# Recurrent gates' pieces before the branch gates' piece, and the first softmax beside the last piece, in a two-layer hybrid decoder on one core

## The reference, cut to what matters

```python
h = x @ W_in            # one projection, columns for all head groups
y = concat([
  nsa_mixer(...),       # 4 heads: compressed + selected + sliding branch, mixed by g = sigmoid(gate_logit)
  sliding_window(...),  # 4 heads with sinks (SWA)
  hgrn2_mixer(...),     # 4 recurrent heads; o = o * rsqrt(mean(o*o) + eps) * norm_g * silu(hg)
]) @ W_out
# compressed branch: blocks = t[:, tok] + cmp_pos ; silu(blocks.reshape(n, 32*64) @ w1) @ w2, for k and for v
```

## Time and profile before

| | |
|---|---|
| median of 3 runs | 2209.33 us (2207.95 to 2210.56) |
| profiled execution, own time | 2208.09 us |
| its span, first to last instruction | 2206.2 us |
| PE busy | 2176.4 us (99%) |
| DVE busy | 1133.1 us (51%) |
| ACT busy | 903.0 us (41%) |
| granted TensorE clock | 1.000 |

### The profile page before, as it was taken

The page is one execution under the profiler, slowest core; times in us unless marked ns, Lnnn a source line. Parts: engine busy times, 40 slices in busy tenths (PEclk is TensorE's granted clock), DMA queues, the critical chain, the costliest instruction groups (busy, mean ns, idle before and its releaser), DMA issues.

```text
span 2206.2 us, 30817 instructions
## 1 busy us (share of the span) xinstructions
PE 2176.4 (99%) x12675; PEld 1801.2 (82%) x12675; DVE 1133.1 (51%) x1968; ACT 903.0 (41%) x1449; POOL 137.5 (6%) x128
## 2 busy tenths in 40 slices
PE   9999999999999999999999999999999999999999
PEld 7888888887668888888888888898876788888888
DVE  4333344898857333343643333358988663333454
ACT  4223223656646322222532222256576463222244
POOL 0000011220000000011000000112200100000110
PEclk9999999999999999999999999999999999999999
DMA  5333333332223333332333333333322233333332
GB/s 169 99 101 97 89 96 91 100 79 58 82 72 87 96 96 96 102 94 85 102 96 97 100 99 87 98 82 100 86 75 62 60 104 96 96 96 105 89 89 72
DMA packets 384220, 202.76 MB, mean 92 GB/s; under 512 B 17361, under 2 KB 381777, under 8 KB 384081
## 3 DMA queue, kind: packets, MB, share of 16 engines
q1 hardware_dynamic: 383520, 200.15, 31.9%
q10 hardware_dynamic: 560, 0.66, 0.1%
HBM read 198.68 MB, written 2.10 MB: 91 GB/s over the span
## 4 chain that ended last, share of the span: by engine, by line
PE 92%; ACT 4%; DVE 3%; issue 1%; DMA 1%; POOL 0%; SPq 0%; DVEq 0%; ACTq 0%
PE banks L254 27%; PE banks L256 27%; PE banks L255 27%; ACT xhi L353 1%; PE banks L1524 1%; ACT xT L354 1%; PE banks L1511 1%; PE banks L1465 1%; PE banks L311 1%; PE banks L305 1%; PE banks L1008 1%; PE banks L306 1%; ACT w_hi L240 0%; PE banks L1012 0%; ACT lev L1720 0%
## 5 line engine op out<-in xcount | busy, mean ns | idle before, releaser
L246 DVE TENSOR_TENSOR w_lo<-w_raw,w_hi 128x1024 fp32r<-128x1024 f32 (+2 forms) x370 | 451.0, 1222 | 814.2 <-ACT w_hi L240 814.0
L254 PE MATMUL banks<-xhi,w_hi 128*128 128x512 f32 (+1 forms) x1936 | 757.2, 391 | 1.5 <-DVE w_lo L246 1.5
L256 PE MATMUL banks<-xhi,w_lo 128*128 128x512 f32 (+1 forms) x1936 | 748.9, 387 | 0.0
L255 PE MATMUL banks<-xlo,w_hi 128*128 128x512 f32 (+1 forms) x1936 | 748.7, 387 | 0.0
L240 ACT ACTIVATE w_hi<-w_raw 128x1024 fp32r<-128x1024 f32 (+2 forms) x370 | 375.9, 1018 | 811.8 <-PE banks L256 796.5
L254 PEld LDWEIGHTS banks<-xhi,w_hi 128*128 128x128 f32 x1936 | 365.0, 189 | 75.9 <-DVE w_lo L246 2.0
L256 PEld LDWEIGHTS banks<-xhi,w_lo 128*128 128x128 f32 x1936 | 363.5, 188 | 74.4
L255 PEld LDWEIGHTS banks<-xlo,w_hi 128*128 128x128 f32 x1936 | 363.8, 188 | 72.7 <-issue 1.0
L254 PE MATMUL banks<-hhi,w_hi 128*128 128x512 f32 (+1 forms) x792 | 293.4, 371 | 0.0
L256 PE MATMUL banks<-hhi,w_lo 128*128 128x512 f32 (+1 forms) x792 | 289.5, 365 | 0.0
L255 PE MATMUL banks<-hlo,w_hi 128*128 128x512 f32 (+1 forms) x792 | 289.4, 365 | 0.0
(11 more groups left out here) (276 smaller groups left out, 1990.8 us busy)
## 6 DMA issues: line engine op xcount, KB each, us to landing
w_raw<-in_ffn_w_gu_dram SPq DMA_DIRECT2D x176, 512.0 KB, 3.9
w_raw<-in_ffn_w_down_dram SPq DMA_DIRECT2D x64, 512.0 KB, 4.0
w_raw<-in_w_in_dram SPq DMA_DIRECT2D x48, 512.0 KB, 4.1
w_raw<-in_ffn_w_down_dram SPq DMA_DIRECT2D x32, 384.0 KB, 3.5
w_raw<-in_w_out_dram SPq DMA_DIRECT2D x32, 256.0 KB, 2.9
w_raw<-in_ple_gate_w_dram SPq DMA_DIRECT2D x16, 512.0 KB, 3.8
w_raw<-in_cmp_k_w_dram SPq DMA_DIRECT2D x16, 256.0 KB, 2.8
w_raw<-in_cmp_v_w_dram SPq DMA_DIRECT2D x16, 256.0 KB, 3.1
```

What stands on the lines that cost most here:

```text
L246: dve.tensor_tensor(part_view(wlo, n), raw_view(split_at[n]).rearrange("p k n -> p (k n)"), part_view(whi, n), ALU.subtract).then_inc(sems ...
L254: pe.matmul(bank, w_hi, x_hi, start=first, stop=False)
L255: pe.matmul(bank, w_hi, x_lo, start=False, stop=False)
L256: return pe.matmul(bank, w_lo, x_hi, start=False, stop=last)
```

## The change

`ORDER` puts the four recurrent-gate pieces at s = 21 to 24 and the branch-gate piece last (s = 25), so ACT moves out s = 21 and DVE moves out s = 25. The gates' tiles move to `lev` 0 to 3. `cut_blocks` runs two steps sooner (s = 21 and 22), as the Silu table's load does by one (s = 22). Three eighths stand before piece 24, three before piece 25 (after `scores(0)`), and two after it; before, two stood before piece 25 and six after it. `gated` of heads 0 to 2 comes in steps 24 and 25. ACT goes from the root of head 3 to the exponentials of unit 0 with no table load between; `scores(1)` comes first after piece 25, in the banks of unit 0. The branch gates' transposes come in turn 1, moved out by a plain copy; their tanh comes in turn 5. Four chunks of eight come sooner, from turns (5, 6, 7, 12, 16, 18, 20, 22) to (2, 4, 6, 7, 12, 15, 18, 21), with the splits of their weights, and chunk 0 waits for each head's part by itself.

```diff
-         T_HI + 3, T_CMP, T_SQ, T_SQ + 1, T_SK, T_Q, T_Q + 1, T_KK, T_VV, T_SV, T_GATE, T_HG, T_HG + 1,
-         T_HG + 2, T_HG + 3]
+         T_HI + 3, T_CMP, T_SQ, T_SQ + 1, T_SK, T_Q, T_Q + 1, T_KK, T_VV, T_SV, T_HG, T_HG + 1, T_HG + 2,
+         T_HG + 3, T_GATE]
...
         def gate_of(h):
-            return lev[:, (0, 1, 12, 13)[h], :]
+            return lev[:, h, :]
...
             for s in range(3, N_IN):
+                if s == N_IN - 2:
+                    pe.wait_ge(*upto("blk_done", layer, 2))
+                    for e in range(3):
+                        eighth(pe, layer, e)
                 if s == N_IN - 1:
                     pe.wait_ge(*upto("rope_out", layer, 3))
                     pe.wait_ge(*upto("swapped", layer, 2))
                     scores(pe, layer, 0)
-                    pe.wait_ge(*upto("blk_done", layer, 2))
-                    eighth(pe, layer, 0)
-                    eighth(pe, layer, 1)
+                    for e in range(3, 6):
+                        eighth(pe, layer, e)
                     square_mean(H - 1)
...
-                if s == LATE:
-                    pe.wait_ge(*upto("b4_out", layer, 4 * H + 1))
-                    projected(pe, layer, T_GATE)
-                    for c in range(QT):
-                        mm = pe.transpose(...)
-                    mm.then_inc(sems["gate_turned"], 1)
...
-                if s == LATE:
+                if s == LATE - 1:
                     act.preload_act_table_set("silu_and_others")
...
-                if s == LATE + 1:
-                    act.wait_ge(*upto("gate_turned", layer, 1))
-                    act.activation(gates[:], src, ACT.Tanh, scale=0.5).then_inc(sems["gates_in"], 1)
...
                 if s == N_IN - 1:
                     act.preload_act_table_set("natural_log_exp_and_others")
                     root(act, layer, H - 1)
-                    act.preload_act_table_set("silu_and_others")
-            act.preload_act_table_set("natural_log_exp_and_others")
+                    exponentials(act, layer, 0)
...
-                if s in (LATE, LATE + 1):
-                    cut_blocks(s - LATE)
-            for g in range(H - 1):
-                gated(dve, layer, g)
+                if s in (LATE - 2, LATE - 1):
+                    cut_blocks(s - LATE + 2)
+                if s == LATE + 1:
+                    gated(dve, layer, 0)
+                    gated(dve, layer, 1)
+                if s == LATE + 2:
+                    gated(dve, layer, 2)
             scaled_head(dve, layer, H - 1)
...
-        CMP_TURNS = {-1: (2, 3), 0: (4,), 1: (5,), 2: (6,), 3: (7,)}
+        CMP_TURNS = {-1: (6, 7)}
+        GATE_TURN = 1
-        HG_HI = {0: (0,), 1: (1,), 2: (2,), 3: (3,)}
-        HG_LO = {1: (0,), 2: (1,), 3: (2,), 4: (3,)}
-        CHUNK_TURNS = (5, 6, 7, 12, 16, 18, 20, 22)
-        SPLIT_TURNS = (3, 4, 5, 10, 14, 16, 18, 20, 21, 22, 23, 24)
+        HG_HI = {0: (0, 1), 1: (2, 3)}
+        HG_LO = {1: (0, 1), 2: (2, 3)}
+        CHUNK_TURNS = (2, 4, 6, 7, 12, 15, 18, 21)
+        SPLIT_TURNS = (0, 2, 4, 5, 10, 13, 16, 19, 21, 22, 23, 24)
...
         def score_bank(n):
-            return 2 - 2 * (n % 2)
+            return 2 if n == 0 else 2 * (n % 2)
...
-            if n >= 2:
+            if n == 1:
+                pe.wait_ge(*upto("exp_done", layer, 1))
+            if n >= 3:
                 pe.wait_ge(*upto("exp_done", layer, n - 1))
-            if n == 1:
+            if n == 2:
                 pe.wait_ge(*chunk_out(layer, N_IN - 1))
                 pe.wait_ge(*chunk_out(layer, N_IN - 2))
...
                 if c == 0:
                     pe.wait_ge(*upto("ms_out", layer, H))
-                    pe.wait_ge(*upto("hg_lo", layer, 4))
...
+                def head_there(k):
+                    pe.wait_ge(*upto("hg_lo", layer, k + 1))
+                multiply(pe, w0 + c, 7, ..., ready=None if c else head_there)
...
+            scores(pe, layer, 1)
             compressed(-1)
             for n in range(UNITS + 4):
                 if n >= 4:
                     values(n - 4)
-                if n + 1 < UNITS:
+                if 0 < n < UNITS - 1:
                     scores(pe, layer, n + 1)
...
+                if n == GATE_TURN:
+                    act.wait_ge(*upto("gate_turned", layer, 1))
+                    act.activation(gates[:], src, ACT.Copy).then_inc(sems["gates_raw"], 1)
                 if n == HID_ACT - 1:
                     act.preload_act_table_set("exp_and_others")
+                    act.wait_ge(*upto("gates_raw", layer, 1))
+                    act.activation(gates[:], gates[:], ACT.Tanh, scale=0.5).then_inc(sems["gates_in"], 1)
```

More of the change, by code:

```diff
@@ L123, in build @@
                 "rope_swap": 24, "rope_step": 6, "rope_out": 6, "swapped": 4,
-                "sv_turned": 1, "sv_out": 1, "gate_turned": 1, "gates_in": 1, "hg_gated": 4, "hg_hi": 4, "hg_lo": 4,
+                "sv_turned": 1, "sv_out": 1, "gate_turned": 1, "gates_raw": 1, "gates_in": 1, "hg_gated": 4, "hg_hi": 4, "hg_lo": 4,
                 "cmp_mm": 8, "hid_odd": 1, "hid_sum": 1, "hid_act": 1, "hid_dve": 1, "hid_turned": 1, "hid_out": 1, "vc_zero": 1, "kc_mm": 1, "kc_out": 6,
@@ L1102, in out @@
                 if gate_:
-                    act.wait_ge(*upto("c_mm", layer, (3 if ORDER[s] < T_HG + 2 else 4) * QT))
+                    act.wait_ge(*upto("c_mm", layer, 3 * QT))
                 act.activation(chunk_tile(s), ps[:, chunk_bank(s), :], ACT.Silu if gate_ else ACT.Copy).then_inc(sems["out_act"], 1)
@@ L1483, in row_max, with exponentials @@
                 dve.tensor_scalar(nb2, m2, -SCALE, None, ALU.mult).then_inc(sems["nb_ready"], 1)
+        def exponentials(act, layer, n):
+            kind, w_ = units[n][0], width(n)
+            act.wait_ge(*upto("nb_ready", layer, n + 1))
+            if n == 1:
+                act.wait_ge(*upto("c_mm", layer, STEPS))
+            if n == 2:
+                act.wait_ge(*upto("hg_gated", layer, H))
+            if kind == SWA:
+                act.activation(e_sink[:, n % 2, :], e_sink[:, n % 2, :], ACT.Exp)
+            for hh in range(2):
+                e = act.activation(prob[n % 3][:, hh, 0:w_], ps[:, score_bank(n) + hh, 0:w_], ACT.Exp, scale=SCALE,
+                                   bias=nb[:, n % 2, hh:hh + 1], accum_out=sums[:, n % 2, hh:hh + 1])
+            e.then_inc(sems["exp_done"], 1)
         def eighth(pe, layer, e):
@@ L1505, in turn @@
                     evicted(n - 1)
+                if n == 0:
+                    pe.wait_ge(*upto("gates_raw", layer, 1))
                 if n == SWA_N:
@@ L1537, in compressed @@
                     eighth(pe, layer, e)
+                if n == GATE_TURN:
+                    pe.wait_ge(*upto("b4_out", layer, 4 * H + 1))
+                    projected(pe, layer, T_GATE)
+                    for c in range(QT):
+                        mm = pe.transpose(ps[:, 4, 32 * c:32 * c + 32], proj[0:32, T_GATE, tokens(c)], ident[0:32, 0:32])
+                    mm.then_inc(sems["gate_turned"], 1)
                 if n == HID_TURN:
-                    pe.wait_ge(*upto("half_done", layer, 3))
+                    pe.wait_ge(*upto("half_done", layer, 4))
                     pe.wait_ge(*upto("hid_dve", layer, 1))
@@ L1563, in compressed @@
                     pe.wait_ge(*upto("pc_done", layer, 1))
-                    pe.wait_ge(*upto("half_done", layer, 4))
+                    pe.wait_ge(*upto("half_done", layer, 5))
                     for u4 in range(4):
@@ L1572, in chunk @@
                     pe.wait_ge(*upto("ms_out", layer, H))
-                    pe.wait_ge(*upto("hg_lo", layer, 4))
                 elif n == SC_TURN + 1:
                     pe.wait_ge(*upto("sc_sub", layer, 1))
-                elif n == PCT_TURN + 2:
+                elif n == PCT_TURN + 1:
                     pe.wait_ge(*upto("pct_out", layer, 1))
@@ L1708, in heads_act @@
                     src = turned_both(m) if units[m][0] == SWA else ps[:, 4:6, 0:width(m)]
-                    if m == 2:
-                        act.wait_ge(*upto("hg_gated", layer, 4))
                     act.activation(prob_t[:, m % 3, :, 0:width(m)], src, ACT.Copy).then_inc(sems["ev_act"], 1)
@@ L1713, in heads_act @@
                     out_hi(ENDS.index(n - 4))
[L1714 to L1722, removed]
+                if 0 < n < UNITS:
+                    exponentials(act, layer, n)
                 between(n)
@@ L1765, in between @@
                     gated(dve, layer, g)
-                if n == 5:
+                if n == HID_ACT:
                     open_gates(dve, layer)
```

6 lines of the change are left out of this document (3 added, 3 removed).

## The result

The change makes the kernel 3.9 us slower: a median of 2213.06 us (2212.28 to 2214.94) against 2209.14 (2207.5 to 2212.45), 16 runs each, ratio 1.0017 with an interval of 1.001 to 1.0025. The direction was the forecast one; the forecast was +5.5.

A forecast was written before the change was run, and what follows sets the result against it. PE is busy 99% of the span, so only its waits count. New waits of 5.85 us a layer, less those removed, gave +2.25 and +3.25, together +5.5: 2214.8 us, range 2208 to 2218.5, likeliest case 2212 to 2217.

The forecast's parts named there:

- Part 1: Before piece 24: eighth 0 waits for DVE's two cuts, late from table load and Silu; 1.05 us a layer.
- Part 2: Eighths 3 to 5 before piece 25: PE waits for their weights' transfers, 0.25 us a layer (0 to 0.45).
- Part 3: After piece 25's end, T, DVE copies before scaling head 3; scores(3) waits for exponentials, 3.45 us a layer (3.0 to 3.9).
- Part 4: First turns, DVE late: chunk 0 waits 0.6 us for the third head, scores(5) waits 0.5 us, each a layer.
- the clock is granted in full: Assumption stated with the sum: PE gets its full clock; no size was given.
- Part 5: Turn 15's chunk covers a wait, minus 1.1 us a layer; turns 23 and 24 wait more, plus 0.5.
- Rival 2: Head 3's scaling runs under piece 25 after all, removing the 3.45 us wait: 3.6 us faster, 2205.7 us; chance 0.1.
- Rival 1: Late DVE catches up: first turns cost nothing, turn 24 gets no worse; 4.5 us new waits a layer, 2211.1; chance 0.2.
- Rival 3: More is late: rotations or probabilities, turns 1 to 4 and 24; some 2 us a layer more, 2219; chance 0.12.
- Rival 4: Nothing measurable changes: waits only move from DMA to DVE one for one, 2209.3 us; chance 0.1.

The follow-up runs named there:

- the first experiment: The changed kernel with DVE's scaling of head 3 moved ahead of the copy of piece 25: 2206.03 us, ratio to before 0.9984.
- turn 15 alone: The kernel before with chunk 4 in turn 15 instead of 16, its split in turn 13 instead of 14: 2206.3 us, ratio 0.9984.
- late chunks: Changed kernel, head 3 scaled and gated before the last copy, second cut before choose, chunks of turns 2, 4, 21 back in 5, 20, 22: 2210.12 us.
- both late: The late chunks kernel with the eighths also where they stood before, two before piece 25 and the rest after: 2208.26 us, ratio to before 0.9997.

## Why the prediction came out as it did

- **Part 1, 1.05 us a layer: right.** 1.02 in both layers. ACT's rows show the load's price too:

```profile
532.47 1.28 ACT L1158 ACT_TABLE_LOAD   x1
533.76 0.60 ACT L1101 ACTIVATE lev<-banks 128x512 f32<-128x512 f32 x1
```

  The Silu follows 0.01 us behind the load, and the wait has the length forecast without a drain. With the 1.38 us that the Trainium skill's page "ScalarE: Activation LUTs", section "What ACT_TABLE_LOAD costs", adds to a load it would have been 2.4, an estimate from that page's figure; the measured 1.02 decides.
- **Part 2, 0.25 (0 to 0.45): the low end held.** No wait on weights is left in either layer.
- **Part 3, 3.45 a layer: right**, 3.36 and 3.35, by the mechanism forecast, and by the first experiment it is the cause and not only its companion. Its sum has a slip: the terms written there (0.7, 3.0, 0.6, 1.15, 1.1) make T + 6.55, not T + 6.75, and so a wait of 3.25. In after the chain from the end of the piece, 559.77, to the fourth scores at 566.40 takes 6.63.
- **Part 4, 0.6 and 0.5: the waits are real but not to be seen in after.** The failed sentence is "the clock is granted in full". The clock fell, cost 2.16 us a layer and covered both waits, 0.70 and 0.29 at full clock. Instead of 1.1 a layer of waiting the place cost 2.16 of slow work.
- **Part 5: right.** Turn 15's wait is gone. Turns 23 and 24 wait 0.65 and 1.67 against 0.41 and 1.33 in before's trace: +0.58, forecast +0.5. The turn that the earlier trace rows doesn't show:

```profile
637.94 0.85 PE L1511 MATMUL banks<-ident,lev 128*128 128x128 f32 x6 [0.41 <-ACT lev L1711]
```

- **The sum: near by luck.** By profile the layers grew by 2.56 and 3.40 against +2.25 and +3.25. But the forecast was all waiting, and PE's waits grew by only 0.83 and 1.78. The clock makes up 2.15 and 2.30 of the rest, the difference in PE's own work between after and the first experiment, whose clock stayed at 1.00. And at full clock that work is shorter in the new order than before, by 0.42 and 0.68 us (101.64 in both layers against 102.06 and 102.32). The prediction had no term for either, and what makes the work shorter is not shown. A miss of 1.4 and 1.5 us in the waits was filled by two terms it had left out.
- **Profiles and medians.** By medians the change costs 3.9, by the profiled executions 6.1, since that of before lay 1.05 under its median and that of after 1.1 above. Both follow the granted clock. Before was timed 65 times in the three batches of the experiments: 14 executions at a mean clock of 1.000 took 2207.2 to 2208.6 us, 22 at 0.998 or less 2209.9 to 2213.9. After's two executions at 0.996, one of them the profiled one, took 2214.2 and 2214.9, its five at 0.998 2212.3 to 2213.3. The prediction started from a profile of before at 1.000, so "the clock is granted in full" fails for a good part of before's executions as well. Where before loses its clock no trace of its own shows; the profile with turn 15 alone shows one place, 567 to 570 us. The forecast lay just above the 0.2%, and the measured effect lies just below it.
- **The rivals.** Rival 2 was not what this kernel does, but is in the main what it does with one call moved: 2206.03, worked out 2205.7. Rival 1's time, 2211.1, is nearly as close to the result as the forecast's, yet its mechanism is refuted: turn 24 got worse, and part 4's place cost something. Rival 3's further lateness did not come: no further wait in turns 1 to 7 in after, and turns 23 and 24 grew by 0.58, not 1.3. Rival 4's exchange one for one is excluded by the ratio's interval.

## What to carry to other kernels

On a queue that keeps its order, look at the first operation behind each wait on the bottleneck engine: whatever stands behind it and doesn't need it is delayed with it; here that made a wait of 3.4 us a layer, and the move of one line was worth 7.0 us. When pieces swap places, ask which engine moves each one out and what used to run in that time. Fill the places where the bottleneck engine catches up with its supplier first, and check that the filler's own buffers are free by then. Read the granted clock beside the waits, and in several executions of the kernel before too: a sum of waits alone misses what the clock takes, and one profile at full clock can be the rare case.

## What the hardware showed that was not expected

TensorE's granted clock fell to 0.50 in the middle of a kernel that keeps it busy 99% of the time. In after this began within a wait of 3.36 us and lasted until about 571.5, some 5 us past its end: the scores and the chunk behind it took 6.07 us instead of 3.91. Three matmul calls (x6 in the row) whose product nobody reads, put into the wait, kept the clock at 1.00 there and made the kernel 1.4 us faster by medians.

A long wait is not needed. With late chunks the longest wait of the first turns was 1.42 us, with turn 15 alone 1.54, with both late 0.96, and each profile has a stretch at 0.50 there all the same: of about 7, 3.5 and 10 us in layer 0. Which of the short waits and short operations in these turns brings it about was not separated.
